# Both prompt halves of the value layer norm: GpSimd in place of VectorE

## The reference, cut to what matters

```python
z = h @ p["w_in"][l]
u, v, q, k, vr, gr, ga, gb = jnp.split(z, ...)
u = jax.nn.gelu(u)
v = layernorm(jax.nn.gelu(v), p["ln_v_g"][l], p["ln_v_b"][l])
a = chunk_spatial_gating(u, v, p["w_s"][l], p["b_s"][l])   # u * (masked 128x128 mix of v)
```

## Time and profile before

| | |
|---|---|
| median of 3 runs | 1657.05 us (1653.19 to 1657.75) |
| the profiled execution | 1657.38 us |
| its span, first to last instruction | 1655.8 us |
| TensorE busy | 1596.0 us, 96% of the span |
| VectorE busy | 865.9 us, 52% |
| ScalarE busy | 272.0 us, 16% |
| GpSimd busy | 46.5 us, 3% |
| mean granted clock of TensorE | 0.987 |

### The profile page before, as it was taken

How to read it: one execution, slowest core, us unless ns; L and a number is a source line. 1 busy time by engine, 2 the same in 40 slices (tenths; PEclk the granted TensorE clock), 3 DMA queues, 4 the chain that set the end, 5 groups by cost and what they waited for, 6 DMA issues and landing times. The chain is left out here.

```text
span 1655.8 us, 24651 instructions
## 1 busy us (share of the span) xinstructions
PE 1596.0 (96%) x9904; PEld 1089.1 (66%) x9904; DVE 865.9 (52%) x1805; ACT 272.0 (16%) x566; POOL 46.5 (3%) x93
## 2 busy tenths in 40 slices
PE   6899999999999999999998999999999999999997
PEld 2699988775698544444458998887648965444443
DVE  2566774565553533443456667656473435344336
ACT  3110001111200331111131100011121032211111
POOL 0000000000100000000000000000010010000000
PEclk8999999999999999999999999999999999999999
DMA  9624657478944649999983246545896452899993
GB/s 399 250 106 153 242 224 286 164 301 340 403 164 150 265 181 410 421 422 420 423 345 141 105 153 251 207 153 204 324 392 275 153 202 102 353 421 420 421 421 150
DMA packets 47042, 451.97 MB, mean 273 GB/s; under 512 B 5632, under 2 KB 5888, under 8 KB 7504
## 3 DMA queue, kind: packets, MB, share of 16 engines
q1 hardware_dynamic: 43200, 409.66, 62.0%
q10 hardware_dynamic: 3456, 37.75, 5.5%
q0 software_dynamic: 272, 2.97, 0.4%
HBM read 411.16 MB, written 39.19 MB: 272 GB/s over the span
## 5 line engine op out<-in xcount | busy, mean ns | idle before, releaser
L758 PE MATMUL ps<-ring,work 128*64 128x512 f32 x1536 | 341.5, 600 | 3.0 <-ACT work L1219 2.7
L758 PEld LDWEIGHTS ps<-ring,work 128*64 128x64 f32 x1536 | 112.1, 138 | 214.8 <-issue 214.6
L758 PE MATMUL ps<-work,ring 128*128 128x160 f32 (+2 forms) x1504 | 235.0, 319 | 6.0 <-DVE work L2012 4.1
L758 PEld LDWEIGHTS ps<-work,ring 128*128 128x128 f32 x1504 | 213.6, 191 | 26.7 <-DVE work L2012 4.4
L1219 ACT ACTIVATE work<-ps 128x256 f32<-128x256 f32 (+6 forms) x238 | 99.5, 437 | 787.9 <-PE ps L758 786.5
L758 PE MATMUL ps<-work 128*128 128x288 f32 (+7 forms) x800 | 191.1, 401 | 7.8 <-ACT work L1219 3.0
L758 PE MATMUL ps<-hT,ring 128*128 128x160 f32 (+2 forms) x1024 | 172.1, 324 | 1.9 <-DVE work L1909 1.9
L758 PEld LDWEIGHTS ps<-work 128*128 128x128 f32 (+2 forms) x800 | 126.7, 186 | 71.1 <-issue 35.7
L758 PE MATMUL ps<-ring,hT 128*32 128x128 f32 (+2 forms) x1776 | 170.7, 313 | 2.4 <-ACT hT L1219 2.4
L758 PEld LDWEIGHTS ps<-hT,ring 128*128 128x128 f32 x1024 | 152.4, 194 | 18.8 <-issue 5.7
L758 PEld LDWEIGHTS ps<-ring,hT 128*32 128x32 f32 (+1 forms) x1776 | 127.0, 132 | 40.0 <-issue 25.8
(11 more groups left out here) (220 smaller groups left out, 1117.6 us busy)
## 6 DMA issues: line engine op xcount, KB each, us to landing
ring<-stream SPq DMA_DIRECT2D x96, 2048.0 KB, 8.9
ring<-stream SPq DMA_DIRECT2D x192, 1024.0 KB, 10.2
state_sample_out<-ring ACTq DMA_DIRECT2D x16, 2048.0 KB, 8.8
state_out<-prm ACTq DMA_DIRECT2D x8, 512.0 KB, 8.8
prm<-params SPq DMA_DIRECT2D x1, 2608.5 KB, 25.2
prm<-params POOLq DMA_DIRECT2D x1, 2608.5 KB, 16.1
cst<-consts SPq DMA_DIRECT2D x1, 1651.0 KB, 18.5
xT<-x_in SPq DMA_DIRECT2D x1, 1152.0 KB, 5.5
```

The lines of the kernel that those rows point to most:

```text
L758: return nc.tensor.matmul(out, lhsT, rhs, start=start, stop=stop, **k)
```

## The change

The six instructions that apply the norm to the prompt halves leave VectorE and are issued by GpSimd instead, with the same shapes. GpSimd now does for each half the inverse root and then the norm; before it did the two inverse roots in a row. VectorE waits in ("lnfold", 0) for the first half to be done, since it overwrites `moments[:, 0, :]` there. The norm of the sample rows stays on VectorE.

```diff
@@ gpsimd
+            def layer_norm(rows, m, gain, offset):
+                pool.drain()
+                pool.tensor_scalar(rows, rows, moments[:, m, 0:1], rstd[:, m:m + 1], ALU.subtract, ALU.mult)
+                pool.drain()
+                pool.tensor_tensor(rows, rows, gain, ALU.mult)
+                pool.drain()
+                pool.tensor_tensor(rows, rows, offset, ALU.add).then_inc(ln_ready, 1)
...
                     if step == ("v", 1):
-                        inverse_root(l, 0)
-                        inverse_root(l, 1)
+                        for tt in range(2):
+                            inverse_root(l, tt)
+                            layer_norm(vn[:, tt, :], tt, R("lng"), R("lnb"))
                         n_var = 2
@@ vector, step ("v", 1)
                         dve.bn_aggr(moments[:, 2, :], stats[:, 0:1, :]).then_inc(fold_ready, 1)
-                        for tt in range(2):
-                            layer_norm(vn[:, tt, :], tt, l, R("lng"), R("lnb"))
                     elif step == ("lnfold", 0):
 
                         out = wait_made(dve, (l, step, "t"))
+                        dve.wait_ge(ln_ready, l * LN_DONE + 1)
                         taken(dve.tensor_copy(moments[:, 0, :], out[:, 0:2]), (l, step, "t"))
```

## The result

The changed kernel takes 1638.01 us, median of 4 runs (1635.6 to 1640.01), against 1657.4 us before (4 runs): a ratio of 0.989, 95% interval 0.9872 to 0.9908. Measured again in five rounds it takes 1638.84 us against 1655.42, a ratio of 0.9905 (0.989 to 0.992), which is 15.7 us off 1655.42. The forecast was 1647.2 us, range 1643 to 1652, so the direction was right and the gain, forecast as 9.8 us, was taken much too small.

A forecast was written before the change was run, and what follows sets the result against it. TensorE's stall ahead of m5 and the slow clock behind it, 8.30 + 8.57 = 16.9 us, bound what could be won; with GpSimd's additions blocking VectorE, 4.7 + 5.1 = 9.8 us off 1657.05 gave 1647.2 us, range 1643 to 1652.

The forecast's parts named there:

- What bounds the kernel: TensorE's stall ahead of m5 of u 0 and the slow clock behind it, in both layers: 16.9 us to win.
- the price of GpSimd's `tensor_scalar`: In GpSimd's norm, one `tensor_scalar` on 128x1024 was put at 1.09 us, taken from L690.
- The bound from above: GpSimd's `tensor_scalar` at 2.34 us instead of 1.09: 0.5 us more in each layer, 1648.3 us.
- The addition itself: GpSimd's addition of two 128x1024 tiles: 2.34 us, scaled from L726; lower bound 1.89 us, upper 4.9 us.
- how long it holds VectorE: VectorE's two-SBUF-input additions, such as L1580, wait for a GpSimd instruction that has begun, for the whole of it.
- the sum of 9.8: Gain of 4.7 us in layer 0 and 5.1 us in layer 1, after the stalls left by GpSimd's additions.
- The block: GpSimd instructions hold VectorE's weight differences for all their time; a partial block, 70% of an addition, would give 1644.4 us.
- The rival "no block at all": GpSimd's additions don't hold VectorE's weight differences: the whole 16.9 us is won, 1640.2 us; chance 0.10.
- The clock: Behind the left stalls of 2.2 and 1.4 us no loss counted; the rival with a loss: up to 1650.9, chance 0.17.
- Late next: The norm's second half runs to about 86 us, the first mix waits for it only at about 97 us.
- The gain given back later: A later stage held by the weight stream gives the time back: 1657.05 us; chance 0.06.
- the dear addition: GpSimd's addition far dearer than L726 says, slower from 4.7 us on: 1661 us at 4.9 us; chance 0.05.

The follow-up runs named there:

- `dve_delay`: Changed kernel with nine batch statistics, about 6.7 us, that nobody reads put on VectorE ahead of the weight difference L1589: 1658.23 us, ratio 1.0014.
- `probe_two`: Changed kernel with more single GpSimd and VectorE instructions behind its end; ran once, time not used: a VectorE addition was held until 1.05 us after a GpSimd `tensor_scalar`'s start.
- `pool_short_scalar`: Changed kernel with GpSimd's `tensor_scalar` cut to the first 256 of 1024 columns: 1642.96 us, ratio 0.9929.
- `dve_both_late`: Kernel before, norm kept on VectorE, both halves moved behind the four weight differences of u 0 and ahead of its `join`: 1644.9 us, ratio 0.9943.
- `pool_scalar_twice`: Changed kernel with GpSimd's `tensor_scalar` done twice in each half, the first time into an unused place: 1650.05 us, ratio 0.9963.
- `dve_scalar`: Changed kernel with the `tensor_scalar` of both halves on VectorE ahead of the weight differences, the additions left on GpSimd: 1648.26 us, ratio 0.9957.
- `dve_split`: Kernel before, norm kept on VectorE, first half moved behind u 0's four weight differences, second behind its `join`: 1636.80 us, ratio 0.9888.

## Why the prediction was wrong

**What bounds the kernel: right.** The stall ahead of m5 and the slow clock behind it, 16.9 us, were all that could be won, and 15.8 of it was won. `dve_delay` puts all of it back.

**The step that failed, first part: the price of GpSimd's `tensor_scalar`.** "I take 1.09 us" comes from L690, which is another operation on one input of the same size; the `tensor_scalar` measured 3.79 us alone. The bound from above was the price of an addition, 2.34 us; so the range was too narrow as well. (For that bound the prediction names 1648.3 us; its own sum gives 0.5 us more in layer 0 and 0.8 us in layer 1, 1648.5.) The addition itself was priced right: 2.34 us predicted, 2.34 to 2.36 measured.

**The step that failed, second part: how long it holds VectorE.** The right price alone would have moved the forecast the wrong way. In layer 0 a `tensor_scalar` from 68.80 to 72.59 that blocks for all of its time would put L1580 at 72.59, m5 at 73.86 and m4 at 82.77, 5.6 us late; in layer 1 m4 would be 5.7 us late. By the prediction's own sum that is about 1652 us, an estimate. Only together with the short hold, about 1.0 of the 3.8 us (`probe_two`), does the price give what was measured.

**What followed from both.** With 1.09 us GpSimd's first addition would have been ready at 70.03, beside a L1580 at 70.18. In truth it is ready 2.6 us behind L1589's start, and L1589 starts 1.3 us behind the `tensor_scalar`, when that holds nothing any more. So L1589 and L1592 pass, and L1594 too, which begins 0.02 us ahead of GpSimd's addition; only L1596 is held, 0.15 us too long for m4. That L1594 passes is luck in part: its lead is 0.02 us here and 0.23 us in layer 1. Behind the addition it would have ended some 2.2 us later, and m7 would have been about 0.8 us late, an estimate from the same rows. `pool_short_scalar` sets the instruction to 1.22 us, so that price and hold are nearly the same, and gets 11.2 us, near the sum of 9.8: the arithmetic of the additions' block holds.

**The block: right for the additions, wrong in its length for the other.** The prediction took each GpSimd instruction to hold VectorE's two-input additions while it lasts. The Trainium skill says so too ("SBUF — State Buffer", Who interferes with whom). For GpSimd's additions the traces agree (3.2 to 3.4 us for a 1.22 us addition); for the `tensor_scalar` they don't, it holds them for about 1.0 of its 3.8 us. Had it held them for all of its time from 66.11 on, L1589 would have started only at 69.90 and m5 would have been 2.4 us late; it was not late at all. One reading of the prediction is a little off: the small additions of the earlier trace rows were not quite alone in layer 1, a GpSimd instruction starts there at 1105.68, 0.17 us before they end.

**The rival "no block at all".** It had 0.10 and 1640.2 us, the time that came nearest, by luck. Its reason was not the right one: the block exists, and the first three weight differences are simply past it.

**The clock.** There was no loss, but the changed kernel doesn't test the forecast: its stalls of 2.2 and 1.4 us never came. Stalls of 0.85 and 1.24 us in `pool_short_scalar` cost no clock (granted clock 1.00 from 69.6 to 78). That one of 1.9 us can cost it is seen in `dve_both_late`, in one of two layers.

**Late next.** On the time axis of the kernel before (2.75 us later than that of this execution) the second half of the norm ended at 88.28 + 2.75 = 91.0 instead of "about 86", and the mix came at 91.67 + 2.75 = 94.4 instead of 97. So the cover was 3.4 us and not the 11 of the prediction's numbers. The second half ended later because of the same price, and because GpSimd's additions wait for VectorE's as well (3.15 to 3.43 us for three of the four). `pool_scalar_twice` shows that this is a real edge. m5 to m4 of ("u", 1) were in time but for 0.21 us.

**The gain given back later:** refuted, the 15.8 us won ahead of the first mix are there in the whole time too. **Slower**, the dear addition: its premise, 4.7 us for an addition, is refuted.

## What to carry to other kernels

When work is moved to another engine because it stands in front of something urgent, try first to leave it where it is and to issue it behind the urgent part: here that gave the same gain, and no engine held another. The new place has to be chosen as well: with both halves ahead of `join` 1644.9 us, with one on each side of it 1636.8. If two engines share an interface, the moment at which each instruction starts counts as much as its length: a longer instruction on GpSimd was harmless and a shorter one cost 4 us. An operation that the trace doesn't show on an engine has no price until it is measured alone; a row of another operation with the same shape was off by a factor of 3.5.

## What the runs showed of the hardware

- GpSimd on 128x1024 float32: `tensor_scalar` with subtract and multiply 3.79 us (per-partition scalars) or 3.63 us (immediates), one multiply 2.79 us, an addition of two tiles 2.34 us. So the `tensor_scalar` forms, with one input, are dearer than the two-input addition, while L690, another one-input operation, takes 1.09 us.
- GpSimd's `tensor_scalar` holds VectorE's additions with two SBUF inputs for its first 0.9 to 1.05 us, GpSimd's addition holds them for about 2.2 of its 2.3 us.
- A waiting GpSimd addition comes in between two VectorE additions in a row. A waiting `tensor_scalar` does not, unless a drain stands between them: 6.86 us behind three in a row, 4.74 us with drains. Each case was seen once in the probes; why the two differ stays open.
- The same 1.9 us stall in front of the same product cost clock in one layer and none in the other, and four stalls of 0.9 to 1.2 us in a row (`dve_scalar`) cost none. The 0.95 us standstill ahead of ("ga", 0) cost clock in layer 0 of the kernel before (4.08 us for 16 matmuls, granted clock 0.58 from 108.2 to 112.3) and none there in `dve_split` (2.41 us). The length of a stall alone does not tell.
